# Two attentions issued by pairs of heads, two parts of a product split during the first mixer, and one weight unit split ahead of a norm

## The reference, cut to what matters

```
x = first_block(...):
    h   = rms_norm(x);  proj = h @ w_in
    mix = concat(attention of 8 heads, pool mixer, gated unit) @ w_out
    x  += rms_norm(mix)
    h   = rms_norm(x);  m = rms_norm(mem)
    q, k, v = h @ wq, m @ wk, m @ wv              # 4 heads of 256
    x  += rms_norm((softmax(q k^T / 16) v) @ wo)
    x  += rms_norm(conv_ffn(rms_norm(x)))          # 1024 -> 2 x 2816 -> 1024
x = second_block(...):
    h   = rms_norm(x);  proj = h @ w_in_2          # ug, c_q, c_kv, qkv, z, ...
    x  += concat(delta rule, sparse attention, conv of 31 taps over ug) @ w_out_2
    q   = rms_norm_per_head(rms_norm(x) @ xa_wq)   # 4 heads of 128
    x  += (softmax(q k^T / sqrt(128)) v) @ xa_wo
    x  += relu(rms_norm(x) @ mlp_w1)^2 @ mlp_w2
```

## Time and profile before

| | |
|---|---|
| median of 3 runs | 961.83 us (961.36 to 965.58) |
| the profiled execution, its own time | 961.84 us |
| its span, first to last instruction | 960.0 us |
| mean granted clock of TensorE, of full speed | 0.963 |
| busy: TensorE, VectorE, ScalarE, GpSimd | 91%, 60%, 43%, 14% |

### The profile page before, as it was taken

One profiled execution on the slowest core, in us unless ns is written; L12 is line 12 of the kernel. 1 busy time (PEld: TensorE's weight loads), 2 busy tenths in 40 slices (PEclk: granted clock), 3 DMA queues, 4 the chain that ended last, 5 costly groups with the idle time before them and its releaser, 6 DMA issues.

```text
span 960.0 us, 13518 instructions
## 1 busy us (share of the span) xinstructions
PE 877.3 (91%) x5610; PEld 774.2 (81%) x5610; DVE 577.4 (60%) x831; ACT 408.6 (43%) x555; POOL 137.1 (14%) x176
## 2 busy tenths in 40 slices
PE   6987998998999999999859978879988889999998
PEld 5985976897899999999548777578767679999996
DVE  4349673536468777766618997666263657555552
ACT  4367233444336544443324553523143445444440
POOL 0150000210100000000207895053000000000000
PEclk9996998998999999999979899899998999999999
DMA  8964344353256565564043423002023138665541
GB/s 286 298 193 140 129 156 152 111 192 115 88 197 217 181 209 185 175 200 152 0 135 119 144 88 132 1 1 89 1 88 124 52 129 267 190 199 182 175 132 44
DMA packets 92344, 136.01 MB, mean 142 GB/s; under 512 B 4435, under 2 KB 76763, under 8 KB 92028
## 3 DMA queue, kind: packets, MB, share of 16 engines
q1 hardware_dynamic: 90428, 129.90, 41.4%
q10 hardware_dynamic: 1120, 2.62, 0.8%
q0 software_dynamic: 736, 2.63, 0.8%
HBM read 133.56 MB, written 1.06 MB: 140 GB/s over the span
## 4 chain that ended last, share of the span: by engine, by line
PE 76%; DVE 14%; ACT 4%; issue 3%; POOL 2%; DMA 2%; SPq 0%; POOLq 0%; DVEq 0%; ACTq 0%
PE work L2042 32%; PE acc L2042 25%; PE work L2497 3%; PE work L1998 3%; DVE split_extra_slot L1379 1%; DVE split_operands L1379 1%; PE work L2019 1%; DMA weight_ring<-in_w_in 1%; DVE arena L1658 1%; ACT hT L906 1%; PE work L2316 1%; PE work L1987 1%; PE work L2296 1%; PE work L2194 1%; PE work L2004 1%
## 5 line engine op out<-in xcount | busy, mean ns | idle before, releaser
L2042 PE MATMUL work<-split_operands 128*128 128x256 f32 x1824 | 223.9, 283 | 4.0 <-DVE split_operands L1379 4.0
L2042 PEld LDWEIGHTS work<-split_operands 128*128 128x128 f32 x1824 | 221.7, 192 | 6.1 <-issue 5.0
L1379 DVE TENSOR_TENSOR split_operands<-weight_ring,split_operands 128x2048 fp32r<-128x2048 f32 x73 | 167.8, 2302 | 94.3 <-ACT split_operands L926 93.8
L2042 PE MATMUL acc<-split_operands 128*128 128x512 f32 x840 | 197.6, 391 | 3.5 <-DVE split_operands L1541 2.5
L2042 PEld LDWEIGHTS acc<-split_operands 128*128 128x128 f32 x840 | 155.9, 188 | 36.4 <-DVE split_operands L1541 2.9
L926 ACT ACTIVATE split_operands<-weight_ring 128x2048 fp32r<-128x2048 f32 x73 | 139.1, 1910 | 103.4 <-PE acc L2042 45.9
L2042 PE MATMUL work<-split_operands,split_extra_slot 128*128 128x256 f32 x1056 | 137.7, 292 | 17.3 <-DVE split_extra_slot L1379 14.7
L2042 PEld LDWEIGHTS work<-split_operands,split_extra_slot 128*128 128x128 f32 x1056 | 135.1, 200 | 19.9 <-issue 16.3
L1379 DVE TENSOR_TENSOR split_extra_slot<-weight_ring,split_extra_slot 128x2048 fp32r<-128x2048 f32 x34 | 78.5, 2310 | 50.8 <-ACT split_extra_slot L926 50.5
L913 ACT ACTIVATE arena<-work 128x512 f32<-128x512 f32 (+1 forms) x68 | 37.6, 559 | 147.0 <-PE work L2042 86.7
L926 ACT ACTIVATE split_extra_slot<-weight_ring 128x2048 fp32r<-128x2048 f32 x34 | 64.9, 1909 | 57.4 <-DMA weight_ring<-in_w_in 19.9
(11 more groups left out here) (310 smaller groups left out, 937.8 us busy)
## 6 DMA issues: line engine op xcount, KB each, us to landing
weight_ring<-in_mlp_w SPq DMA_DIRECT2D x32, 1024.0 KB, 5.5
weight_ring<-in_w_up SPq DMA_DIRECT2D x22, 1024.0 KB, 5.1
weight_ring<-in_w_in SPq DMA_DIRECT2D x20, 1024.0 KB, 6.5
weight_ring<-in_w_down SPq DMA_DIRECT2D x11, 1024.0 KB, 4.8
weight_ring<-in_w_out SPq DMA_DIRECT2D x8, 1024.0 KB, 4.8
weight_ring<-in_w_mk SPq DMA_DIRECT2D x4, 1024.0 KB, 6.2
weight_ring<-in_w_mv SPq DMA_DIRECT2D x4, 1024.0 KB, 5.4
weight_ring<-in_w_mq SPq DMA_DIRECT2D x4, 1024.0 KB, 4.9
```

The source lines that it names most:

```text
L1379: dve.tensor_tensor(slot[:, 1, :], weights(split_units[i], 2048), slot[:, 0, :], ALU.subtract).then_inc(low_ready, 1)
L2042: ins = pe.matmul(out, lhs(p), rhs(q), start=(start and n == 0), stop=(stop and n == 2))
```

## The change

1. `ug0` leaves `WHOLE`. ScalarE and VectorE split it ahead of the post norm behind `down`, and TensorE runs it by `split_pair`. The slots of this phase are named in the other order, so that the units behind it keep theirs.
2. VectorE takes the low rows of `memkv` ahead of the low parts of the weights `mk`.
3. `out`: the high and low parts of columns 2 and 3 are made while the attention still runs. After it TensorE first does both units for rows 0 to 127, then both for the other rows, then units 0 and 1 by row tile.
4. The memory attention goes by pairs of heads, and the queries of the second pair stand between the scores of the first and their turned probabilities.
5. The second attention too: `xq` 1 is taken head by head, the sums go to accumulator banks, VectorE adds the small constant and GpSimd takes the power -1/2, one activation ahead of it touches the exponential, and the first unit of `xwo` is cut into three pieces, which stand between the parts of the second pair.

The diff, cut to its core:

```diff
-WHOLE = ("q0", ("mk", 2), ("mk", 3), "ug0", ("xq", 0), ("m1", 0))
+WHOLE = ("q0", ("mk", 2), ("mk", 3), ("xq", 0), ("m1", 0))
...
             act.wait_ge(mix_tail, 1)
             act.wait_ge(*drained(("pool_out",)))
-            for c in MIX_ORDER:
-                high_mix("out", c, mixT[:, 2 * c:2 * c + 2, :] if c >= 2 else
-                         acc(("o", c))[:, :].rearrange("p (c t) -> p c t", c=2))
+            for c in MIX_ORDER[:2]:
+                high_mix("out", c, mixT[:, 2 * c:2 * c + 2, :])
+            for c in MIX_ORDER[2:]:
+                act.wait_ge(*acc_filled(("o", 1)))
+                high_mix("out", c, acc(("o", c))[:, :].rearrange("p (c t) -> p c t", c=2))
             high_parts(upto(("mq", 1)))
...
-                    act.wait_ge(neg_max, m)
+            for hp in range(2):
+                if hp:
+                    high_parts(upto(("wo", 2)))
+                    drain_queries(3)
+                for t in range(TT):
+                    act.wait_ge(neg_max, TT + 2 * hp + t + 1)
                     for j in range(2):
                         h = 2 * hp + j
                         ins = act.activation(mprobs[t][:, h, :], bank(("ms", t, hp))[:, SEQ * j:SEQ * j + SEQ], ACT.Exp,
                                              bias=msoft[:, t, 0, h:h + 1], accum_out=msoft[:, t, 1, h:h + 1])
                     ins.then_inc(reader(("ms", t, hp)), 1)
-            high_parts(upto(("wo", 2)))
             for c in range(4):
                 high_mix("wo", c, halves(("mo", c)), full(("mo", c)))
             high_parts(upto(("up", 1)))
...
                 if j >= 1:
                     gate_gelu(j - 1)
+            high_parts(upto("ug0"))
             post_squares("down", "down_post")
             next_squares("mix2", 4)
...
             drain_cross_values(0)
             high_rows("mix2")
-            high_parts(upto("ug0"))
             drain_cross_values(1)
...
+            def cross_exps(hp):
+                for t in range(TT):
+                    if hp == 1 and t == 1:
+                        high_mix("xwo", 0, halves(("xo", 0)), full(("xo", 0)))
+                    act.wait_ge(x_max, 2 * hp + t + 1)
                     for j in range(2):
                         h = 2 * hp + j
                         ins = act.activation(xprobs[t][:, h, :], bank(("xs", t, hp))[:, SEQ * j:SEQ * j + SEQ], ACT.Exp,
...
+            cross_queries(0, 2, ("xq", 0), 0)
+            cross_queries(2, 1, ("xq_head", 2), 0)
+            cross_exps(0)
+            cross_queries(3, 1, ("xq", 1), 0)
+            cross_exps(1)
             high_parts(upto(("m1", 0)))
-            for c in range(2):
-                high_mix("xwo", c, halves(("xo", c)), full(("xo", c)))
+            high_mix("xwo", 1, halves(("xo", 1)), full(("xo", 1)))
...
                         if j == 0:
                             ins.then_inc(first_max, 1)
                     ins.then_inc(reader(name), 1)
-                low_parts(upto(("mk", 0)) + t)
                 for half in range(2):
                     low_rows("memkv", t, half)
+                low_parts(upto(("mk", 0)) + t)
             name = ("pool_out",)
...
                     low_parts(upto(("out", MIX_ORDER[int(h == 5)])))
+                if h in (5, 7):
+                    c = MIX_ORDER[int(h == 7)]
+                    low_mix("out", c, mixT[:, 2 * c:2 * c + 2, :]).then_inc(acts_low, 1)
...
+                low_mix("wo", c, bank(("mo", c))[:, :].rearrange("p (c t) -> p c t", c=2)).then_inc(reader(("mo", c)), 1)
+
+            memory_maxima(0)
+            memory_weights(0)
+            low_parts(upto(("wo", 1)))
+            for t in range(TT):
+                memory_turned(t, 0)
+            memory_maxima(1)
+            memory_weights(1)
+            memory_lows(0)
+            memory_turned(0, 1)
+            memory_lows(1)
+            memory_turned(1, 1)
             low_parts(upto(("wo", 2)))
-            for c in range(4):
-                low_mix("wo", c, bank(("mo", c))[:, :].rearrange("p (c t) -> p c t", c=2)).then_inc(reader(("mo", c)), 1)
+            for c in range(2, 4):
+                memory_lows(c)
...
+            low_parts(upto("ug0"))
             post_norm("down", "down_post", 3)
...
+            def cross_means(hp):
+
+                dve.wait_ge(*acc_filled(("xq_sums", hp)))
+                dve.tensor_scalar(xq_root[:, hp], acc(("xq_sums", hp))[:, 0:4].rearrange("p (t j) -> p t j", t=TT),
+                                  P * EPS, None, ALU.add).then_inc(acc_read, 1)
...
+
+            cross_means(0)
+            cross_maxima(0)
+            for t in range(TT):
+                cross_weights(t, 0)
+            cross_means(1)
+            for t in range(TT):
+                cross_turned(t, 0)
+            cross_maxima(1)
+            cross_weights(0, 1)
+            cross_lows(0)
+            cross_turned(0, 1)
+            cross_weights(1, 1)
+            cross_turned(1, 1)
             low_parts(upto(("m1", 0)))
-            for c in range(2):
-                low_mix("xwo", c, bank(("xo", c))[:, :].rearrange("p (c t) -> p c t", c=2)).then_inc(reader(("xo", c)), 1)
+            cross_lows(1)
...
+            early, pair = MIX_ORDER[:2], MIX_ORDER[2:]
+            for t in range(TT):
+
+                pe.wait_ge(acc_read, FILL[("out", 2 * t + 1)] - 3)
+                for n, c in enumerate(early):
+                    if t == 0:
+                        pe.wait_ge(*low_there(("mix", "out", c)))
+                        pe.wait_ge(low_ready, SPLIT[("out", c)] + 1)
+                    w = split_weights(("out", c), 2, D)
+                    for kk in range(2):
+                        for half in range(2):
+                            ins = split_matmul(acc(("out", 2 * t + half))[:, :],
+                                               lambda p: mix_part("out", p, c)[:, kk, P * t:P * t + P],
+                                               lambda p: w[:, p, kk, 512 * half:512 * half + 512], n == 0 and kk == 0, False)
+                    if t == TT - 1:
+                        ins.then_inc(unit_spent, 1)
+            split_last_units([("out", c) for c in pair], False,
+                             lambda n, p, kk, t: act_s["out"][p][:, 2 * pair[n] + kk, P * t:P * t + P],
+                             lambda n: low_there(("mix", "out", pair[n])))
...
+
+            for c in range(2):
+                pe.wait_ge(*drained(("mk", c)))
+                pe.wait_ge(*drained(("mq", c)))
+            memory_scores(0)
+            split_pair(("mq", 3), "mem")
+            memory_probs(0)
+            for c in range(2, 4):
+                pe.wait_ge(*drained(("mk", c)))
+                pe.wait_ge(*drained(("mq", c)))
+            memory_scores(1)
+            pe.wait_ge(*acc_drained(("mv", 3)))
+            for t in range(TT):
+                pe.wait_ge(*drained(("mpT", t, 0)))
+            for c in range(2):
+                memory_mixed(c)
+            memory_probs(1)
+            open_product("wo")
+            pe.wait_ge(*low_there(("mix", "wo", 0)))
+            split_product_unit(("wo", 0), True, False, wo_rows(0))
+            for t in range(TT):
+                pe.wait_ge(*drained(("mpT", t, 1)))
+            for c in range(2, 4):
+                memory_mixed(c)
+            pe.wait_ge(*low_there(("mix", "wo", 1)))
+            split_product_unit(("wo", 1), False, False, wo_rows(1))
+            split_last_units([("wo", c) for c in (2, 3)], False,
+                             lambda n, p, kk, t: act_s["wo"][p][:, 2 * (2 + n) + kk, P * t:P * t + P],
+                             lambda n: low_there(("mix", "wo", 2 + n)))
...
             norm_T("mix2", 10)
             cross_values(1)
-            drained_norm("mix2")
-            pair_of_chunks(("ug0",), "ug0")
             rows_split("mix2")
+            split_pair(("ug0",), "mix2", "ug0")
...
+            def cross_sums(hp):
+
+                ps = acc(("xq_sums", hp))
+                for t in range(TT):
+                    for j in range(2):
+                        at = 2 * t + j
+                        ins = pe.matmul(ps[:, at:at + 1], xq_sq[:, 2 * hp + j, P * t:P * t + P], conc("ones")[:, 0:1],
+                                        start=True, stop=True)
+                ins.then_inc(acc_full, 1)
+
...
+            pe.wait_ge(*acc_drained(("out2", 3)))
+            pe.wait_ge(*drained(("xq", 0)))
+            cross_sums(0)
+            cross_scores(0)
+            split_chunk(("xq", 1), ("xq", 1), "cross", 1)
+            for t in range(TT):
+                cross_probs(t, 0)
+            pe.wait_ge(*drained(("xq_head", 2)))
+            pe.wait_ge(*drained(("xq", 1)))
+            cross_sums(1)
+            cross_scores(1)
+            for t in range(TT):
+                pe.wait_ge(*drained(("cross_v", t)))
+            cross_mixed(0)
+            cross_probs(0, 1)
+
+            def xwo_steps(c, steps):
+                return split_steps(("xwo", c), c == 0, c == 1,
```

(17 more changed lines are left out.)

223 lines of the change are left out of this document (107 added, 116 removed).

## The result

The changed kernel takes 937.31 us in the median of 4 runs (935.84 to 938.67), against 963.71 us (961.36 to 966.77, 4 runs) for the kernel before. The ratio is 0.9736 with a 95% interval of 0.9717 to 0.9755. The profiled execution took 937.43 us, 24.4 us less than the 961.84 of the profile before; its span is 935.7 us, where it was 960.0. I had forecast 31.8 less (930.0) and a range of 925 to 941.

What follows compares the result with a forecast made beforehand. Only TensorE's 83 us of waits and its busy time at half clock could give time back; 3.7 + 4.3 + 5.9 + 13.3 + 4.6 = 31.8 off 961.8 gave 930.0 us, range 925 to 941.

Steps and rivals of the forecast that it cites:

- My own case: Whole kernel: the gains of the five parts come as summed, 926 to 934 us; chance 0.64.
- A: First memory keys: low rows ahead of low weights shorten the wait by 2.2 and restore clock for 1.5; 3.7 us.
- B: `out`, first mixer's product: early units remove the 3.31 wait and slow first products; 4.3 us after a later post norm.
- my 13.7 us: At `out`: unit 2's slot becomes free 13.7 us ahead of the product's end, in place of 16.4.
- C: Memory attention by pairs: no waits or half clock left, 7.5 us saved, less 1.6 for a later post norm; 5.9.
- I put 1.6 us on that: Post norm behind `wo`: later because ScalarE's copy of `up` 1 ends only 1.6 us ahead of the product's end.
- D: Behind the third norm: `ug0` split, `ug1` loaded early and run right behind it; 13.3 us.
- my own list: Signs of a wrong prediction: `cq` waited for, clock 0.5 inside C or E, D's gain given back in the convolution.
- E: Second attention by pairs, to the end of `xwo`: 4.6 of 33.8 us saved.
- the first two together: Rivals: clock still falls at A, C or E (934 to 936); loads or copies return as waits (935 to 945); together 0.25.
- The rival on the other side: Ahead of the third norm: `ug0`'s copy, its load landing late, blocks ScalarE before the squares; chance 0.02.
- The half of C's loss that I hung on one row: Post norm behind `wo`: GpSimd's first operation takes 1.01 us beside VectorE's subtraction, not 0.18; 0.83 us moves with it.

Runs made afterwards that it cites:

- squares_first: Changed kernel with copies of `mq` 1 and `up` 1 moved from ahead of post norms' squares (ScalarE) and post norms (VectorE) to between their row halves: 930.93 us.
- squares_no_pairs: `squares_first` with the memory attention of the kernel before, not by pairs of heads: 936.63 us.
- no_memory_pairs: Changed kernel with only the memory attention by pairs of heads undone: 937.2 us.
- low_late: `squares_first` plus warming products in TensorE's waits, with VectorE's low part of `up` 1 moved behind the `ffn` norm's drain: 928.82 us.

## Why the prediction was right, and where it was off

The time lies in the range, and the mechanisms of the five parts hold. My own case had 926 to 934, though, and that isn't what came: 937.3 was reached through losses that I had only as rivals, and the falls of the clock came at other places than those I named. That the time is inside the range owes something to luck. By its steps:

- **A, 3.7.** Right in both terms. Undone it costs 3.0 to 3.9, and the keys' half clock went with the wait.
- **B, 4.3.** Right: 4.1 in the profiles of before and after; undone it is 3.3 in the profile and 3.9 to 4.8 by the medians. Within it, the post norm was late by 1.3 instead of my 0.8, and the product itself gained 5.3. The slot of unit 2 becomes free after 36 of the 96 products, not after 60 as I wrote; my 13.7 us are right, since they count the 60 that are left.
- **C, 5.9.** Its first term, 7.5 to the end of `wo`, was measured as 7.4. The step that failed is the one I wrote as "I put 1.6 us on that": it was 4.7. I had ScalarE's copy of `up` 1 end 1.6 us ahead of the product's end; it ended 0.2 behind it, 1.8 later than I had. With the 1.3 of lower clock named below, which I hadn't counted there, that is the 3.1. The load took 7.61 us, where my 5.8 is that of the profile before. It was issued at 237.50, and the load ahead of it in the queue only 2.2 us earlier, since two low parts are now made back to back; in the profile before 5.1 us lie between the two. Both were in flight at once and landed after 7.0 and 7.6 us. The queue's own timeline and a window of the profile after show it (the window's fifth number is the DMA share, the last GB/s):

```profile
235.30 0.37 SPq L736 DMA_DIRECT2D weight_ring<-in_xa_wkv  x1
```

```profile
238.00:240.00 2.00, 2.00 (x10) 1.00 1.07 375
240.00:242.00 2.00, 2.00 (x11) 1.00 1.07 353
```

  That the overlap makes them slow is read from these rows and wasn't tried by itself. The later norms then left TensorE waiting 3.4 us, and the clock was low for the next 3 us, which is another 1.3. `squares_first` and `squares_no_pairs` show the copy's place in ScalarE's queue as the cause: with it moved, the pairs are worth some 5 us.
- **C, what it is measured against.** Of the 7.5 us, 2.0 were the half clock in the results. `no_memory_pairs` gets them back without the pairs. I had counted that term as the part's. Whether it went with A and B or with the execution isn't known: there is one profile of before.
- **D, 13.3.** Right: 13.4 for `ug0` and `ug1` in the profiles, 13.7 to 14.6 undone. `cq` was the next to be late, as I wrote: its load took 7.3 us and TensorE waited 0.2. By my own list a wait for `cq` is a sign against the prediction; at 0.2 us it is about what I had given for a load of over 7.2. The 1.7 in the memory values lie ahead of it and don't belong to the split.
- **E, 4.6.** The mechanism is right, and the size is 5.6. My term for the wait at the second pair's weights was 1.1, and it was 0.7; the added 0.4 for the pieces' waits and the short waits before were nearly nothing: the two halves of the scores, transposes and results follow each other with no gap in the timeline up to 728.2. GpSimd's power took 1.01 and 1.02 us, where I took 0.56 and had 1.01 as a bound; no link of the chain that ended last is a power.
- **The rivals.** What came is the first two together, within the 945 that I gave: loads and copies that come back as a wait (3.1 and the 0.5 at B), and a clock that falls (1.7 and 1.7, and 1.4 in the inputs), though inside none of the three places that I named, A, C and E. The rival on the other side didn't come: `ug0`'s copy and subtraction were done before the squares behind `down`.
- **GpSimd and VectorE.** The half of C's loss that I hung on one row was no chance: the operation took 0.81 to 1.08 us beside the subtraction, and 0.19 without it. `low_late` shows that moving the subtraction away is what changes it. By the Trainium skill's page "SBUF — State Buffer", in its section on the two sides of SBUF, the two exclude each other at a shared port, and this trace agrees.

## What to carry to other kernels

When a product is made to end earlier, ask first for what stands ahead of the norm in the queue of the engine that starts it: a copy that waits for a load holds back work that was ready 5 us ago, and a part worth 5 us then shows as 0. Undo one part and put it in again on top of the repair before calling it worthless. And price a wait of 1 to 3 us on TensorE with the 1.5 to 3 us that the products behind it may lose to the lower clock: fill it with products of no use where idle time is certain. That filling pays was shown at one place, `xq` 0. Read a loss or a gain from the stretch that was edited, too: here the profiles carry 1 to 3 us from elsewhere.

## What the runs showed of the hardware that wasn't expected

The same program with the same waits can have TensorE at 2.4 GHz in one execution and at 1.2 GHz for some us in another: the changed kernel had a granted clock of 0.50 from 48 to 52 us in one profile, straight behind windows in which it was busy all the time, and 1.00 in the other, and its keys started 1.3 us later for it. With waits of 1.1 and 1.6 us ahead of `xq` 0 the clock fell ten times in ten; with 0.22 and 0.64, filled by two products of 0.94 us, it fell in neither of two. What decides at the places between, the memory values and `m1` 0, stays open, and so does the slow first unit (7.14 to 9.41 us with a granted clock of 1.00).

A GpSimd operation on 128x1 that began beside VectorE's subtraction of 128x2048 ended 0.05 or 0.06 us behind it in all eleven profiles where the two met behind `wo`, and took 0.19 us in the one where they didn't.
